# Hyena's spectra and x1 issued by SyncE and its tables first on GpSimd; in the tail, the norm factor computed inside the modulation

## What is computed

```python
def _fftconv(u, hf, bias):
    L = u.shape[1]
    U = jnp.fft.rfft(u, n=2 * L, axis=1)
    y = jnp.fft.irfft(U * hf[None], n=2 * L, axis=1)[:, :L]
    return y + u * bias

# Hyena, order 2, 512 channels, context and latent as separate sequences
z = x1 * _fftconv(v, hf[:, 0], hy_bias[0])
o_hy = x2 * _fftconv(z, hf[:, 1], hy_bias[1])
...
# the tail
x = x + gate1 * (merged @ w_out)
h2 = _rmsnorm(x, norm2_g) * (1.0 + scale2) + shift2
x = x + gate2 * (jnp.square(jax.nn.relu(h2 @ w_up)) @ w_down)
return rmsnorm(x)
```

## Time and profile before

| | us |
|---|---|
| median of 3 runs | 2893.49 |
| lowest, highest | 2892.32, 2897.98 |
| the profiled execution | 2890.1 |
| its span | 2888.3 |
| busy: PE, DVE, ACT, POOL | 2707.6 (94%), 1273.6 (44%), 895.7 (31%), 803.8 (28%) |
| mean granted clock of PE | 0.961 of full |

### The profile page before, as it was taken

One profiled execution on the slowest core, in us unless ns is written; L12 is line 12 of the kernel. 1 busy time (PEld: TensorE's weight loads), 2 busy tenths in 40 slices (PEclk: granted clock), 3 DMA queues, 4 the chain that ended last, 5 costly groups with the idle time before them and its releaser, 6 DMA issues. The chain is left out here.

```text
span 2888.3 us, 36192 instructions
## 1 busy us (share of the span) xinstructions
PE 2707.6 (94%) x14803; PEld 2318.0 (80%) x14803; DVE 1273.6 (44%) x1882; ACT 895.7 (31%) x1500; POOL 803.8 (28%) x551
## 2 busy tenths in 40 slices
PE   9687999999999999999898699798999999999998
PEld 7566887788888898888677588587888888888886
DVE  7566664445565445444876511326211212212215
ACT  2342221045555455554211421214122121121121
POOL 3546984111001010100233033213232232232230
PEclk9778999999999999999999799899999999999999
DMA  6666775442213221311756432501111111111101
GB/s 199 215 209 235 227 229 194 146 155 94 95 54 114 101 95 53 110 70 69 250 187 226 179 115 113 213 30 37 37 37 37 38 43 37 37 37 37 44 23 73
DMA packets 101858, 324.75 MB, mean 112 GB/s; under 512 B 12337, under 2 KB 30355, under 8 KB 101310
## 3 DMA queue, kind: packets, MB, share of 16 engines
q1 hardware_dynamic: 75678, 230.68, 23.2%
q0 software_dynamic: 26016, 91.76, 9.4%
HBM read 237.99 MB, written 76.02 MB: 109 GB/s over the span
## 5 line engine op out<-in xcount | busy, mean ns | idle before, releaser
L89 PE MATMUL tl_b<-tl_hi,tl_whi 128*128 128x512 f32 (+1 forms) x960 | 344.9, 359 | 21.2 <-DVE tl_lo L2447 15.3
L90 PE MATMUL tl_b<-tl_lo,tl_whi 128*128 128x512 f32 (+1 forms) x960 | 342.6, 357 | 0.0
L91 PE MATMUL tl_b<-tl_hi,tl_wlo 128*128 128x512 f32 (+1 forms) x960 | 341.7, 356 | 0.0
L2388 DVE SCALAR_TENSOR_TENSOR tl_x<-tl_b,all_mod,tl_x 128x512 f32<-128x512 f32 (+1 forms) x216 | 142.5, 661 | 375.1 <-PE tl_b L91 362.8
L2282 POOL TENSOR_TENSOR tl_wlo<-tl_raw,tl_whi 128x1024 fp32r<-128x1024 f32 x72 | 178.3, 2478 | 445.5 <-ACT tl_whi L2201 445.5
L89 PE MATMUL tl_b<-tl_uhi,tl_whi 128*128 128x512 f32 (+1 forms) x768 | 275.1, 358 | 3.5 <-POOL tl_ulo L2292 3.5
L91 PE MATMUL tl_b<-tl_uhi,tl_wlo 128*128 128x512 f32 (+1 forms) x768 | 276.6, 360 | 0.0
L89 PE MATMUL at_out<-h_hi,at_whi 128*128 128x424 f32 (+1 forms) x672 | 263.9, 393 | 12.8 <-POOL at_wlo L510 10.9
L90 PE MATMUL tl_b<-tl_ulo,tl_whi 128*128 128x512 f32 (+1 forms) x768 | 274.5, 357 | 0.0
L695 DVE TENSOR_REDUCE at_nmax<-at_s 128x1 f32<-128x1280 f32 (+1 forms) x160 | 196.8, 1272 | 111.9 <-PE at_s L562 111.3
L510 POOL TENSOR_TENSOR at_wlo<-at_raw,at_whi 128x1024 fp32r<-128x1024 f32 x28 | 66.2, 2363 | 626.5 <-ACT at_whi L611 626.5
(11 more groups left out here) (295 smaller groups left out, 5777.3 us busy)
## 6 DMA issues: line engine op xcount, KB each, us to landing
tl_raw<-in_w_tail SPq DMA_DIRECT2D x72, 512.0 KB, 3.7
hy_tab<-in_hy_tab POOLq DMA_DIRECT2D x68, 512.0 KB, 4.9
hd_wa<-in_w_adaT SPq DMA_DIRECT2D x32, 512.0 KB, 4.3
at_raw<-in_w_proj SPq DMA_DIRECT2D x28, 512.0 KB, 4.6
fd_in<-in_xT SPq DMA_DIRECT2D x16, 640.0 KB, 4.6
s_gatesT<-at_pad SPq DMA_DIRECT2D x16, 640.0 KB, 2.9
...
```

Source lines behind the costliest of these rows:

```text
L89: pe.matmul(out, w_hi, x_hi, start=first, stop=False)
L90: pe.matmul(out, w_hi, x_lo, start=False, stop=False)
L91: return pe.matmul(out, w_lo, x_hi, start=False, stop=last)
L2388: dve.scalar_tensor_tensor(out=x1[:, n, at:at + m], in0=bank[x % GEMM_BANKS][:, 0:m], scalar=g.mod[:, gate, SEG_OF[c]:SEG_OF[c] + 1], in1= ...
```

## The change

In Hyena SP issues the spectra; POOL's list holds tables and bias parts only, and each table's issue depends on nothing but its own slot. SP's list is: spectra 0 and 1, two tiles of x1, the bias, spectra 2 to 9, the other two tiles of x1 (after all of `fwd_read` of order 0), and, once x1 is turned, spectra 10 to 19. In the inverse half POOL loads two tables ahead of the bias parts and six behind the first two of them. PE turns x1's tile i-1 in the middle of inverse tile i (behind its second part), and the last tile behind tile 1 of order 1's first forward runs.

In the tail, `scale_of` and `deviation` of chunk j+1 stand inside `modulate` and `shift` of chunk j, ahead of k = 4, and `spread_out` of chunk j+1 behind k = 6 of PE's UP matmuls of chunk j; the sums for the last chunk are taken behind k = 1 of the second chunk. ACT rectifies the first two UP jobs ahead of the last `shift`. In the last group the UP jobs too go in `C_ORDER`, and each DOWN waits for `u_l` by that order.

```diff
@@ -1474,19 +1474,6 @@
...
-def units_before(o, j=None, tile=None):
...
@@ -1529,13 +1516,28 @@
...
         def _(sp):
+            def load_spec(n):
+
+                o, j = divmod(n, FTILES)
+                if n >= 2:
+                    sp.wait_ge(fwd_read, n - 1)
+                sp.dma_start(spec[n % 2][:, 0:spectra(j)], g.spec[o, j, :, 0:spectra(j), :]
+                             ).then_inc(spec_in[n % 2], 16)
+
             sp.wait_ge(tab_in[2 * TOGETHER - 1], 16)
-            sp.dma_start(bias[:], g.d["hy_bias"]).then_inc(bias_in, 16)
+            for n in range(2):
+                load_spec(n)
             for c in range(2, CHT):
                 sp.dma_start(x1[c][:], g.convT[CHT + c]).then_inc(x1_in, 16)
+            sp.dma_start(bias[:], g.d["hy_bias"]).then_inc(bias_in, 16)
+            for n in range(2, FTILES):
+                load_spec(n)
             sp.wait_ge(fwd_read, FTILES)
...
                 sp.dma_start(x1[c][:], g.convT[CHT + c]).then_inc(x1_in, 16)
+            sp.wait_ge(x1_turned, HT)
+            for n in range(FTILES, 2 * FTILES):
+                load_spec(n)
...
@@ -1603,6 +1605,8 @@
...
                             turn_v(n)
+                    if o and tile == 1:
+                        turn_x1(HT - 1)
                 for j in range(TOGETHER, FTILES):
...
@@ -1636,8 +1640,8 @@
...
                         mm.then_inc(runs, 1)
-                    if o == 0:
-                        turn_x1(i)
+                        if o == 0 and i and x == 1:
+                            turn_x1(i - 1)
...
@@ -1679,48 +1683,37 @@
...
         def _(pool):
-            def load_spec(n):
-
-                o, j = divmod(n, FTILES)
-                if n >= 2:
-                    pool.wait_ge(fwd_read, n - 1)
-                pool.dma_start(spec[n % 2][:, 0:spectra(j)], g.spec[o, j, :, 0:spectra(j), :]
-                               ).then_inc(spec_in[n % 2], 16)
-
             def load_table(m):
...
-            for m in range(2 * TOGETHER):
-                load_table(m)
-            for m in range(2):
-                load_spec(m)
-            for m in range(2 * TOGETHER, TAB_SLOTS):
+            def biased_tile(n):
+                o, i = divmod(n, HT)
+                if i >= 2:
+                    pool.wait_ge(zdone, n - 1)
+                else:
+                    pool.wait_ge(g_lo, 2 * (o + 1) * FTILES)
+                for h in range(2):
+                    m = pool.tensor_tensor(scr[n % 2][:, 2 + h], z[h][:, i], bias[:, o], ALU.mult)
+                m.then_inc(biased, 1)
+
+            for m in range(TAB_SLOTS):
                 load_table(m)
             for o in range(2):
-                for j in range(FTILES):
-                    for m in units_before(o, j=j):
-                        load_table(m + TAB_SLOTS)
-                    if j + 2 < FTILES:
-                        load_spec(o * FTILES + j + 2)
+                for u in range(FWD_U + 2):
+                    load_table(o * NU + u + TAB_SLOTS)
                 if o == 0:
                     pool.wait_ge(bias_in, 16)
-                pool.wait_ge(g_lo, 2 * (o + 1) * FTILES)
-                for i in range(HT):
-                    n = o * HT + i
-                    if i >= 2:
-                        pool.wait_ge(zdone, n - 1)
-                    for m in units_before(o, tile=i):
-                        load_table(m + TAB_SLOTS)
-                    for h in range(2):
-                        m = pool.tensor_tensor(scr[n % 2][:, 2 + h], z[h][:, i], bias[:, o], ALU.mult)
-                    m.then_inc(biased, 1)
-                if o == 0:
-                    pool.wait_ge(x1_turned, HT)
-                    for n in range(FTILES, FTILES + 2):
-                        load_spec(n)
+                for i in range(2):
+                    biased_tile(o * HT + i)
+                for u in range(FWD_U + 2, FWD_U + 8):
+                    load_table(o * NU + u + TAB_SLOTS)
+                for i in range(2, HT):
+                    biased_tile(o * HT + i)
+                    for u in range(FWD_U + 4 * i, min(FWD_U + 4 * i + 4, NU)):
+                        load_table(o * NU + u + TAB_SLOTS)
...
@@ -2105,7 +2098,7 @@
...
         else:
-            jobs += [(UP, up + k, k, c) for k in range(GT) for c in range(NC)]
+            jobs += [(UP, up + k, k, c) for k in range(GT) for c in (range(NC) if i < GROUPS - 1 else C_ORDER)]
         if i < GROUPS - 1:
...
@@ -2127,6 +2120,7 @@
...
     SQ = LATE + 2 * NC
+    SCALE_AT, SUMS_AT, SPREAD_AT = 4, 1, 6
     with stage(nc, "tl") as st:
...
@@ -2218,18 +2212,25 @@
...
                 for k in range(KD):
+                    if j < NC - 1 and k == SCALE_AT:
+                        deviation(0, j + 1)
                     act.wait_ge(xa_done, j * KD + k + 1)
...
                                    bias=g.mod[:, SHIFT2 + k, SEG_OF[c]:SEG_OF[c] + 1]).then_inc(h_h, 1)
+
+            def relu_of(x):
+                m, o = CHUNKS[JOBS[x][3]][1], UPS_TO[x]
+                act.wait_ge(mm, x + 1)
+                if o >= 2:
+                    act.wait_ge(u_l, o - 1)
+                act.activation(r[o % 2][:, 0:m], bank[x % GEMM_BANKS][:, 0:m], ACT.Relu).then_inc(relu, 1)
...
                 o = UPS_TO[x]
-                act.wait_ge(mm, x + 1)
                 if o >= 2:
-                    act.wait_ge(u_l, o - 1)
-                act.activation(r[o % 2][:, 0:m], bank[x % GEMM_BANKS][:, 0:m], ACT.Relu).then_inc(relu, 1)
+                    relu_of(x)
                 act.wait_ge(squared, o + 1)
...
@@ -2252,13 +2253,14 @@
...
                     square(0, LATE + 2 * j + n - LATE, n, columns(c))
-                    if j and n == LATE:
-                        deviation(0, j - 1)
+                    if j == 1 and n == LATE:
+                        deviation(0, 0)
                 if j:
...
                 freed(x)
-            deviation(0, NC - 1)
+            for x in range(FIRST_UP, FIRST_UP + 2):
+                relu_of(x)
             shift(NC - 1)
...
@@ -2318,8 +2320,10 @@
...
                 free(x)
-                if kind == DOWN:
-                    pe.wait_ge(u_l, UPS_TO[x] - (NC - 1 - c if n == 0 and x < FIRST_LAST else 0))
+                if kind == DOWN and x < FIRST_LAST:
+                    pe.wait_ge(u_l, UPS_TO[x] - (NC - 1 - c if n == 0 else 0))
+                elif kind == DOWN:
+                    pe.wait_ge(u_l, UPS_TO[x] - (NC - 1 - C_ORDER.index(c)))
                 deep = GT if kind == DOWN else KD
...
@@ -2350,8 +2354,8 @@
...
                     token_sums(0, j - 1, LATE + 2 * j)
-                if j >= 1 and n == 1:
-                    spread_out(0, j - 1)
+                if j == 1 and n == 1:
+                    spread_out(0, 0)
             for k in range(2):
...
@@ -2362,9 +2366,10 @@
...
                         accumulate(x + s, k, k == 0, k == KD - 1)
-                if j == 0:
-                    token_sums(0, NC - 1, SQ)
-                    spread_out(0, NC - 1)
+                    if (j, k) == (1, SUMS_AT):
+                        token_sums(0, NC - 1, SQ)
+                    if j < NC - 1 and k == SPREAD_AT:
+                        spread_out(0, j + 1)
             for x in range(FIRST_UP + 2 * NC, len(JOBS)):
...
@@ -2417,6 +2422,8 @@
...
                     q = j * KD + k
+                    if j < NC - 1 and k == SCALE_AT:
+                        scale_of(0, j + 1)
                     if k < KD:
...
@@ -2457,14 +2464,13 @@
...
                     sum_up(0, LATE - 1, slice(0, T), False)
-                else:
-                    scale_of(0, j - 1)
+                elif j == 1:
+                    scale_of(0, 0)
                 add(x + 1)
...
                     modulate(j - 1)
-            scale_of(0, NC - 1)
             modulate(NC - 1)
...
```

9 lines of the change are left out of this document (removed).

## The result

| | before, us | after, us |
|---|---|---|
| median | 2892.9 (4 runs) | 2860.15 (4 runs) |
| lowest, highest | 2887.02, 2897.98 | 2854.52, 2860.7 |
| the profiled execution, its span | 2890.1, 2888.3 | 2860.7, 2858.9 |
| PE's mean granted clock | 0.961 | 0.966 |

The ratio is 0.9881, 95% interval 0.9868 to 0.9895: 32.7 us or 1.1% faster. Forecast were 2854 and a range of 2845 to 2866. So the sign and the size held, and the forecast was 6 us too hopeful.

The account below looks back on a forecast made before the run. PE, busy 94% of the span, was taken as the bound, with the gain in its gaps: Hyena 28.2, tail's head 6, last group 5.1, sum 39.3 us off 2890.1; with 3.4 for the median, 2854, range 2845 to 2866.

Parts of the forecast that it names:

- A: Hyena, order 0's first forward: PE's 3.92 us wait for a late table and its slow stretch go; gain 6.2 us.
- E: Hyena, order 1's j = 9: PE, now earlier, waits 3.6 us for DVE, plus 2.0 slow clock; cost 4.4 us.
- B: Hyena, first turn of x1: waits of 4.25 and 0.93 us and 3.4 of slow clock go; gain 8.6 us.
- C: Hyena, change of order: the 2.31 us wait for the last z_M and 1.6 of slow clock go; gain 3.9 us.
- D: Hyena, order 1's forward: 3.96 us table wait, 1.8 slow clock and a 0.66 wait go; gain 6.4 us.
- F: Hyena, order 1's inverse: the 5.82 us wait for a late table and 1.7 of slow clock go; gain 7.5 us.
- Tail's head: Start of the tail: first UP matmuls start earlier, but POOL holds the third modulation 2 to 3 us; gain 6 us.
- Last group: Tail's last group: the 3.51 us wait for POOL's low part and 1.6 of slow clock go; gain 5.1 us.
- (1): All gaps go, DVE isn't late at order 1's j = 9, third modulation isn't held: 2847 or 2845; chance 0.12.
- (2): Tables and x1 land late in Hyena, costing half or a third of its gain: 2868 or 2863; chance 0.18.
- (3): The tail's head nets nothing, short PE waits bringing slow stretches: 6 us less, 2860; chance 0.10.
- (4): Slower: in order 1's forward PE runs from short wait to short wait at 1.2 GHz, 2898; chance 0.03.

Follow-up runs that it names:

- old_turns: Changed kernel with x1's transposes back behind each inverse tile; ratio to the kernel before 0.9890, Hyena stretch 217.2 us.
- tab_late: Changed kernel with POOL's inverse-half tables issued as before, behind the wait for `g_lo`, spectra still on SP; ratio to the kernel before 0.9921, Hyena stretch 227.2 us.
- tab_mid: Changed kernel with one more table ahead of POOL's bias parts and others between them; ratio to the kernel before 0.9875, Hyena stretch 211.2 us.
- short_dve: Changed kernel without two of DVE's eight operations per frequency tile, so its output lacks a term; ratio to the kernel before 0.9840, Hyena stretch 203.1 us.
- after_again: The changed kernel timed once more, code unchanged; ratio to the kernel before 0.9871, median 2857.11 us, tail's head 72.4 us.

## Why the prediction was right, and where it was off

- **A** (6.2): the table wait went altogether. From the first forward matmul to the first inverse one, 55.2 us became 47.7, 7.5, 1.3 more than forecast; where that 1.3 comes from stays open. But 1.86 us, with a slow stretch (clock 0.61; 9 matmuls in 3.24 us, 1.3 lost), came back in the inverse as a wait for DVE's low part. The step that failed: E's argument, that a PE made faster meets DVE, was made for order 1 and not for order 0.
- **B and C** (8.6 and 3.9): the waits for hy_x and z_M went. Order 0 from its first forward matmul to order 1's took 118.3 us before and 102.8 after, 15.5. Of that 0.8 is the eight transposes that moved into order 1, so 14.7 stand for the 18.7 of A, B and C. Against the terms stand the 1.86 with its 1.3, and a table wait of 1.19 behind POOL's two bias parts, an item that the prediction didn't price and that breaks its own sign of no table wait over 1. As prices of the moved turns the two terms were too high. Their slow stretches, 3.4 and 1.6, don't follow from the waits (in old_turns both waits came back and the clock stayed full), and B had the late table down as 0.93, where tab_late shows 7.38 once x1's wait no longer stands over it. The sum came near because the same change moved the tables too. The margin of 0.9 for x1 held in after and gave way in tab_mid.
- **D and E** (6.4 less 4.4): order 1's forward, 55.5 to 54.0, with eight transposes (0.8 us) moved in: 2.3, forecast 2.0. E's mechanism stood, at 4.81 for 3.6 us of wait; behind it 13 matmuls at half clock, 2.6 us (5.4 less 13 x 0.217), for 2.0. About half of those 13 fall behind the end of the forward half and so into F, which is one reason why the net here still fits with the longer wait. short_dve showed the cause.
- **F** (7.5): 57.9 to 51.3, 6.5, the slow stretch behind E reaching into it. tab_late, with 4.20 of wait back in order 1, showed that the place of the first tables does it. (The prediction calls F's 1.7 of slow clock D's, but D's is 1.8.)
- **Tail's head** (6): 7.3, or 8.7 in executions like after_again. The waits came nearly as worked out; the hold of the third modulation was mis-sized, 1.7 for 2 to 3. The prediction's working has a slip there too: 1978 and 6.9 and 2 to 3 give 1986.9 to 1987.9, not 1986.8 to 1987. That the head gained more than forecast made up for a part of Hyena's shortfall, which is luck.
- **Last group** (5.1): 5.2 and 5.3.
- **Rivals.** DVE wasn't on time (1); landings had medians of 4.8 (tables) and 5.8 (x1), about as before, so transfers didn't come late (2); the head gained well more than nothing (3); DVE-bound waits stayed one per half and PE's clock full between them, which is what the last rival was to decide (4).
- **The sum**: 36.0 of 39.3 in the stretches. The median's gain was 32.7; the rest is within what the start, 1356 to 1372 us, makes of 4 runs.
